# 118 instead of 108 of chunk 0's v rows in its own stage, weight loads ahead of two stores, the last sum in two halves

## What is computed

```python
xn = RMSNorm(h)
experts, gates = top16_of_product_keys(xn @ wq)         # per head: 16 ids, softmax of their scores
act = gelu(einsum('chkd,cd->chk', u_tab[experts], xn))  # 128 dots per token
y   = h + einsum('chk,chkd->cd', gates * act, v_tab[experts])
```

## Time and profile before

| | |
|---|---|
| median of three runs | 2894.3 us |
| the profiled execution | 2897.38 us, of which span 2895.4 us |
| PE busy | 2580.4 us (89%) |
| DVE busy | 2115.7 us (73%) |
| POOL busy | 1982.2 us (68%) |
| ACT busy | 871.6 us (30%) |
| DMA engines, mean | 389 GB/s over the span, 1125.04 MB |
| chain that ended last | PE 36%, DMA 20%, issue 20%, POOL 16%, DVE 5% |

### The profile page before, as it was taken

The page is one execution under the profiler, slowest core; times in us unless marked ns, Lnnn a source line. Parts: engine busy times, 40 slices in busy tenths (PEclk is TensorE's granted clock), DMA queues, the critical chain, the costliest instruction groups (busy, mean ns, idle before and its releaser), DMA issues.

```text
span 2895.4 us, 29720 instructions
## 1 busy us (share of the span) xinstructions
PE 2580.4 (89%) x7557; PEld 1169.3 (40%) x7557; DVE 2115.7 (73%) x5274; ACT 871.6 (30%) x2016; POOL 1982.2 (68%) x2061
## 2 busy tenths in 40 slices
PE   8999978989978898899979998799989999777777
PEld 4544434434523344344523444244523444222222
DVE  5788876967886678777887778777887757744444
ACT  3223331342214421253214521264214631111111
POOL 1026567677777777777777777777777777777775
PEclk9999989999999999999999999999999999999999
DMA  6239999999999999999999999999999999999999
GB/s 241 96 137 383 349 417 378 340 419 419 419 419 412 411 419 419 419 412 414 413 413 406 407 419 419 411 386 417 419 419 403 395 413 419 414 420 419 419 419 370
DMA packets 321344, 1125.04 MB, mean 389 GB/s; under 512 B 35937, under 2 KB 43641, under 8 KB 321176
## 3 DMA queue, kind: packets, MB, share of 16 engines
q0 software_dynamic: 294912, 1073.87, 92.1%
q1 hardware_dynamic: 26248, 49.27, 4.8%
q10 hardware_dynamic: 16, 0.00, 0.0%
HBM read 1114.62 MB, written 8.39 MB: 388 GB/s over the span
## 4 chain that ended last, share of the span: by engine, by line
PE 36%; DMA 20%; issue 20%; POOL 16%; DVE 5%; ACT 2%; POOLq 0%; ACTq 0%; DVEq 0%
PE psum L1720 17%; POOL w_kept L1621 9%; DMA w_kept<-in_peer_u,experts 9%; PE psum L521 9%; DMA ring_v<-in_peer_v,experts 9%; POOL ring_v L1621 7%; PE psum L1129 3%; DMA w_kept<-in_peer_v,experts 2%; PE psum L1103 2%; PE psum L1652 2%; DVE w_kept L2039 2%; PE psum L1680 1%; PE psum L1670 1%; DVE acc L959 0%; PE psum L1147 0%
## 5 line engine op out<-in xcount | busy, mean ns | idle before, releaser
L1720 PE MATMUL psum<-ring_v,diag 128*128 128x512 f32 x3244 | 1562.7, 606 | 248.8 <-DMA ring_v<-in_peer_v,experts 160.9
L2039 DVE CUSTOM_DVE_ANT_0 w_kept<-w_kept,psum 128x1024 f32<-128x1024 f32 x928 | 1125.5, 1218 | 534.9 <-DMA w_kept<-in_peer_u,experts 529.0
L1621 POOL DMA_INDIRECT w_kept<-in_peer_u,experts x928 | 891.7, 961 | 322.1 <-issue 244.2
L1621 POOL DMA_INDIRECT ring_v<-in_peer_v,experts x841 | 809.9, 963 | 276.1 <-issue 222.2
L1720 PEld LDWEIGHTS psum<-ring_v,diag 128*128 128x128 f32 x3244 | 564.8, 190 | 1022.9 <-issue 754.0
L1866 ACT ACTIVATE diag<-ident,weights 128x128 f32<-128x128 f32 x974 | 353.2, 393 | 739.0 <-PE psum L1720 582.3
L1720 PE MATMUL psum<-w_kept,diag 128*128 128x512 f32 x652 | 315.9, 609 | 40.6 <-DMA w_kept<-in_peer_v,experts 24.7
L521 PE MATMUL psum<-w_sb,xnT 128*128 128x512 f32 x640 | 284.6, 600 | 0.8 <-ACT xnT L701 0.8
L470 POOL DMA_INDIRECT w_kept<-in_peer_u,experts x96 | 90.1, 939 | 230.5 <-DVE experts L1389 177.5
L1621 POOL DMA_INDIRECT w_kept<-in_peer_v,experts x183 | 181.6, 992 | 66.0 <-issue 48.3
L1995 DVE SCALAR_TENSOR_TENSOR acc<-conv_in,taps,acc 128x128 f32<-128x128 f32 x720 | 205.0, 347 | 0.0
(11 more groups left out here) (246 smaller groups left out, 1760.7 us busy)
## 6 DMA issues: line engine op xcount, KB each, us to landing
w_kept<-in_peer_u,experts POOLq DMA_INDIRECT x1024, 9.9
ring_v<-in_peer_v,experts POOLq DMA_INDIRECT x841, 10.2
w_sb<-in_w_in SPq DMA_DIRECT2D x4, 2048.0 KB, 17.0
x_in<-in_x SPq DMA_DIRECT2D x8, 512.0 KB, 6.7
w_kept<-in_w_out SPq DMA_DIRECT2D x1, 4096.0 KB, 14.5
h_res<-in_x SPq DMA_DIRECT2D x8, 512.0 KB, 7.2
w_kept<-in_peer_wq SPq DMA_DIRECT2D x2, 2048.0 KB, 10.4
wo_sb<-in_w_out SPq DMA_DIRECT2D x1, 4096.0 KB, 23.6
```

Of the source, the lines that this page charges most:

```text
L1621: nc.gpsimd.indirect_dma_start(slot(kind, n), None, peer_u[0] if kind == "u" else peer_v[0], bass.IndirectOffsetOnAxis(S.experts[c % 2][:, ...
L1720: last = nc.tensor.matmul(y_ps[:, j * BANK:(j + 1) * BANK], diag[:, e % DIAGS, :], slot("v", n)[:, j * BANK:(j + 1) * BANK], start=e == 0, ...
L2039: nc.vector.tensor_tensor_reduce(out=row, in0=row, in1=hn, scale=1.0, scalar=0.0, op0=ALU.mult, op1=ALU.add, accum_out=dots[:, e:e + 1]).t ...
```

## The change

In phase 0, for the last chunk, the two weight loads are issued ahead of `store_h` and `store_q`: `wo_sb` once TensorE has finished group Q (before: G, but behind `store_h`), `wq_sb` once it has finished K. In phase 1, `CAUGHT` becomes 118: ten more v rows of chunk 0 in its own stage, and slots 0 to 9 of stage 1 issue only u rows; v rows 118 to 127 follow in slots 10 to 19. Of chunk 0's v rows 49 instead of 43 go aside, of the last 20 rows of the kernel 10 instead of 7. Chunk 0's head 7 is weighed at slot 47 of its own stage. `end_y` and the last store are made in two halves of 512 columns.

```diff
--- before.py
+++ after.py
@@ -427,6 +427,11 @@
             at = slice(n * BANK, (n + 1) * BANK)
             sp.dma_start(w_kept[:, :, at], peer_wq[0, :, at].rearrange("(k p) n -> p k n", p=P)).then_inc(landed, 16)
         for i in range(2, CHUNKS):
+            if i == LAST:
+                sp.wait_ge(projected[Q], CHUNKS)
+                sp.dma_start(wo_sb[:, :, :], w_out[0].rearrange("(k p) n -> p k n", p=P)).then_inc(S.wo_loaded, 16)
+                sp.wait_ge(projected[K], CHUNKS)
+                sp.dma_start(wq_sb[:, :, :], peer_wq[0].rearrange("(k p) n -> p k n", p=P)).then_inc(S.wq_loaded, 16)
             store_h(i)
             if i == LAST - 2:
                 sp.wait_ge(S.tapped, 2 * TAPS * CB)
@@ -434,12 +439,7 @@
                 sp.dma_start(conv_in[:, :, :], hT_spill[:, :, 2 * P:3 * P + HALO]).then_inc(S.c_in, 16)
             if i < LAST - 1:
                 next_x(i + 1)
-            if i == LAST:
-                sp.wait_ge(projected[G], CHUNKS)
-                sp.dma_start(wo_sb[:, :, :], w_out[0].rearrange("(k p) n -> p k n", p=P)).then_inc(S.wo_loaded, 16)
             store_q(i)
-        sp.wait_ge(projected[K], CHUNKS)
-        sp.dma_start(wq_sb[:, :, :], peer_wq[0].rearrange("(k p) n -> p k n", p=P)).then_inc(S.wq_loaded, 16)
         sp.wait_ge(qT_stored, 16 * CHUNKS)
         sp.wait_ge(hT_stored, 16 * CHUNKS)
 
@@ -1442,15 +1442,15 @@
     side_added = sem("side_added")
     FIRST, TAIL = 0, CHUNKS - 1
     AT_ONCE = 8
-    CAUGHT = ROWS - LAG
+    CAUGHT = 118
     kept = range(EARLY + AT_ONCE, ROWS)
     apart = len(kept) - 0
     u_slot = {e: 2 * n if n < apart else 42 + 4 * (n - apart) for n, e in enumerate(kept)}
     first_u = {at: e for e, at in u_slot.items()}
-    head_ends = {u_slot[(h + 1) * TOPK - 1] + 1: h for h in range(AHEAD, PH - 1)}
+    head_ends = {u_slot[(h + 1) * TOPK - 1] + 1: h for h in range(AHEAD, PH)}
     first_at = {4 + e * (SLOTS - 5) // CAUGHT: e for e in range(CAUGHT)}
-    SIDE = ([row_of(FIRST, e) for e in range(CAUGHT) if (e % 3 != 0 if 30 <= e < 70 else e % 4 == 3)]
-            + [row_of(TAIL, e) for e in range(ROWS - LAG, ROWS) if e % 3 == 0])
+    SIDE = ([row_of(FIRST, e) for e in range(CAUGHT) if (e % 3 != 0 if 30 <= e < 56 else e % 4 != 0 if 56 <= e < 76 else e % 4 == 3)]
+            + [row_of(TAIL, e) for e in range(ROWS - LAG, ROWS) if e % 2 == 0])
     FIRST_SIDES = len([n for n in SIDE if n < ROWS])
     y_side = w_kept[:, KT_D - 2, :]
     in_side = lambda c, e: row_of(c, e) in SIDE
@@ -1494,6 +1494,8 @@
 
         if c == FIRST:
             return (FIRST, first_at[s]) if s in first_at else None
+        if c == FIRST + 1 and s < CAUGHT - (ROWS - LAG):
+            return None
         return (c, s - LAG) if s >= LAG else (c - 1, s - LAG + ROWS)
 
     def rows_in_order():
@@ -1519,7 +1521,10 @@
 
         if c == FIRST and s < SLOTS - LAG + SPREAD:
             return (FIRST, first_at[s + LAG - SPREAD]) if s + LAG - SPREAD in first_at else None
-        return (c, s - SPREAD) if s >= SPREAD else (c - 1, s - SPREAD + ROWS)
+        e = s - SPREAD if s >= SPREAD else s - SPREAD + ROWS
+        if c == FIRST and e < CAUGHT or c == FIRST + 1 and s < SPREAD and e < CAUGHT:
+            return None
+        return (c, e) if s >= SPREAD else (c - 1, e)
 
     def heads_ended(c, s):
 
@@ -1578,8 +1583,11 @@
                 store(c - 1)
 
         over_chunks(step)
-        store(CHUNKS - 1)
-        sp.wait_ge(y_stored, 16 * CHUNKS)
+        for j in range(2):
+            at = slice(j * BANK, (j + 1) * BANK)
+            sp.wait_ge(y_copied, 2 * (CHUNKS - 1) + j + 1)
+            sp.dma_start(out[0, (CHUNKS - 1) * P:, at], y_out[:, at]).then_inc(y_stored, 16)
+        sp.wait_ge(y_stored, 16 * (CHUNKS + 1))
 
     @block.gpsimd
     def _(pool):
@@ -1921,7 +1929,7 @@
         def step(c, f):
             for s in range(SLOTS):
                 if c is not None:
-                    if s == 0 and later(c):
+                    if s == 0 and c > FIRST + 1:
                         gelu(c - 1, PH - 1)
                     for w in heads_ended(c, s):
                         gelu(c, w)
@@ -2077,10 +2085,15 @@
 
         def end_y():
 
-            dve.wait_ge(row_added, pe_rows(CHUNKS * ROWS - 1))
             dve.wait_ge(side_added, len(SIDE))
             dve.wait_ge(y_stored, 16 * (CHUNKS - 1))
-            nc.vector.tensor_tensor(y_out[:, :], y_ps, y_side, ALU.add).then_inc(y_copied, 2)
+            for j in range(2):
+                at = slice(j * BANK, (j + 1) * BANK)
+                if j == 0:
+                    dve.wait_ge(half_added, CHUNKS)
+                else:
+                    dve.wait_ge(row_added, pe_rows(CHUNKS * ROWS - 1))
+                nc.vector.tensor_tensor(y_out[:, at], y_ps[:, at], y_side[:, at], ALU.add).then_inc(y_copied, 1)
 
         def front(f, s):
             a, after = divmod(s - ATT0 - ATT_SUM, ATT_STEP)
@@ -2147,7 +2160,7 @@
                     u, v = u_at(c, s), v_at(c, s)
                     if u is not None:
                         dot_row(c, u)
-                    if s == 1 and later(c):
+                    if s == 1 and c > FIRST + 1:
                         weigh_rows(c - 1, PH - 1)
                     if s:
                         for h in heads_ended(c, s - 1):
```

## The result

The changed kernel takes 2908.7 us (median of five runs, 2905.2 to 2909.6) against 2892.8 for the kernel before (median of five, the three named at the start among them): 1.0045 times its time, 95% interval 1.0034 to 1.0055. By that ratio it is **13 us slower**; the two medians lie 16 us apart, and 27 and 23 further runs of the kernel before, beside the experiments, have medians of 2894.1 and 2894.6 us. The forecast was 2891.4 with a range up to 2898. It was wrong in sign and in range.

What follows compares the result with a forecast made beforehand. It took gathers, paced nearly equally by DMA and POOL, to bound the kernel. On the span, +9.8 - 12.5 + 1.0 - 1.2 = -2.9 us gave a median forecast of 2891.4 us, range 2884 to 2898.

Steps and rivals of the forecast that it cites:

- What bounds the kernel: Whole kernel: DMA and POOL paces nearly equal, 1.25 and 1.24 us a gather; gathers that start earlier shorten it.
- Part 1: Weight loads ahead of the stores, end of phase 0: v row 3 held until 381, v row 12 late by 3.3 us.
- Part 2: Ten more v rows in stage 0: +13.8, -2, +1.8 us; chunk 1 starts 9.8 us later, then -12.5 us for fewer gathers.
- the hole would close: End of stage 0: experts ready at 567.7 just as POOL arrives, first u row of chunk 1 at 569.1.
- Part 3: Slots 0 to 9 of stage 1, u rows alone: waits for dots cost +1 us, between 0 and 5.5.
- Part 4: Head 7 weighed at once: two instructions change place on engines with idle time, worth nothing.
- Part 5: Kernel's end: last add and store in halves, -1.2 us, between 0 and -1.5; the changed rows aside cost nothing.
- The rivals: Four other outcomes: waits vanish 2887.3 (chance 0.29), stores don't wait 2882 (0.05), hole stays 2893.8 (0.09), slower 2904 (0.10).
- the slower one: Rival at v row 3 of chunk 0: `store_h` lands at up to 394, POOL 16 us late, 2904 us; chance 0.10.

Runs made afterwards that it cites:

- e3: The kernel before with only the two weight loads moved ahead of both stores; 2897.4 us, 1.0009 of the kernel before.
- g3: The kernel before with only `wo_sb` ahead of the last `store_h`, `wq_sb` behind both stores, last add and store in halves; 2887.7 us, 0.9975 of the kernel before.
- e1: The changed kernel with all 13 buffers open to v rows from row 44 of chunk 0 instead of 40; 2898.0 us, 1.0011 of the kernel before.
- g4: The kernel before with all 13 buffers open to v rows from row 36 of chunk 0 instead of 40; 2911.8 us, 1.0062 of the kernel before.
- h1: The changed kernel with `wo_sb` ahead of the last `store_h`, `wq_sb` behind both stores, all 13 buffers from row 49; 0.9967 of the kernel before, at some 355 GB/s.
- g2: The changed kernel with all 13 buffers from row 44 and the weight loads behind the stores as before; 2898.3 us, 1.0009 of the kernel before.
- g1: The changed kernel itself, unaltered, run again; 2907.6 us, 1.0042 of the kernel before.

## Why the prediction was wrong, step by step

**What bounds the kernel**: right. Gathers that POOL starts sooner or later are the time: the changed kernel's last v gather starts 8.9 us later than before (2889.88 against 2880.98), its span is 7.7 us longer, and the difference is the 1.2 us of the halves.

**Part 1**: right in size. v row 3 held until 380.61 (forecast 381), v row 12 at 399.70, +4.2 us (forecast +3.3); timed alone it costs 2.6 us (e3). `wq_sb` took 34.5 us from its issue at 343.33 and `store_h` 30.8 from 349.04, so they landed at 377.8 and 379.8. The trace agrees with the rule of the Trainium skill (DMA: Bandwidth & Descriptors, Queues, rings and completion order) that each DMA engine takes the descriptors of one queue in ring order. What I missed is that the order could be halved: with one load ahead of the store (g3) v row 3 is held for 1.57 us and the kernel is faster, with both it is held for 17.39 and the kernel is slower.

**Part 2** is the step that failed. It said that POOL's extra idle in stage 0 "shrinks as POOL comes later than before: -2 us". The two new waits alone are 7.04 + 4.96 - 0.60 = 11.4 us over the usual gaps. From v row 12 to the last v row of the stage, the waits of 0.9 us and more add up to 4.0 us over the gaps before (1.17, 2.53, 1.22) and 12.2 after (with 1.15): **+8.2 us instead of -2**. The other terms were right or better: part 1 +4.2 (forecast +3.3), and what is left for the ten gathers is 12.1, where the sum had 13.8 + 1.8 = 15.6, so that error hid 3.5 us of the other one. Together the last v row starts 24.5 us later (575.48 against 551.00); the forecast had 16.9. I had costed ten gathers, six rows aside and four more on TensorE, and I had asked of the buffers at the start of chunk 1 whose rows they hold. I did not ask it of the other end of the same stretch, although `first_at` and `ALONE` stand in the text: one number, `CAUGHT`, moves row 40 from slot 49 to 45, and the other, 40, stays. So the first gather of chunk 1 started at 577.38 instead of 569.1, 8.3 us off, and e1 gives some 10 us back. g4 puts the same kind of stall into the kernel before, where it costs 18, its third wait included.

The forecast that the hole would close was right: the experts stand at 576.10 and POOL comes just then. It closed because both came late.

**Part 3** was taken too low: +1 us, between 0 and 5.5. The waits at chunk 1's start are 0.96 + 1.68 + 2.66, 4.4 us over the usual gaps, and the stage of chunk 1 became 9.0 us shorter, not 11.5. The last two, 3.7 us over the gaps, are the mechanism I named: u rows 6 and 9 of chunk 1 wait for the dots of rows 0 and 3, whose buffers they take, and h1 has the same two. In e1 and g2 they are absent, and POOL waits for TensorE instead (g2: 7.0 us over the gaps), for the buffers of the last v rows, which I had put "inside the same bound". Without the loads the sum gave the ten rows 9.8 - 3.3 - 12.5 + 1.0 = -5.0 us, and waits of this size are enough to use that up. That the rows would pay without them is not shown.

**Part 4**: nothing, as far as a profile shows. **Part 5**: 1.2 us in the profile, as forecast; not to be timed. **The rivals**: the slower one had its place at v row 3, with a landing at 390. The landing was at 379.8 and the slowness came 80 us later, by another wait.

## What to carry to other kernels

When rows are packed closer in a schedule with a shared ring of buffers, compute for each end of every stretch who held the buffer, and how many gathers lie between; a gather that takes the buffer of the one two before it costs a landing and a use, with the whole in-order queue behind it. A hole at the end of a stage is no stock of time: a stall in the middle delays the engine that ends the hole too. When a load is moved ahead of a store to fill idle DMA time, ask who waits for the store, and count the bytes ahead of it: here 4 MB ahead gained some 7 us (halves of the last sum included), and 8 MB lost 3. Where between them it turns wasn't measured.

## What the runs showed of the hardware that I had not expected

An issue on SP can itself last long. Behind the two weight loads the instruction of `store_h` took 4.19 us and that of `store_q` 11.93, against 0.53 and 0.33 before:

```profile
343.33 0.38 SPq L434 DMA_DIRECT2D wq_sb<-in_peer_wq  x1
349.04 4.19 SPq L398 DMA_DIRECT2D hT_spill<-hT_out  x1
353.27 11.93 SPq L393 DMA_DIRECT2D qT_spill<-qT_out  x1
```

In e1, e3 and g1, with the same order of loads, they took 4.88 to 6.31 and 10.30 to 11.42 us. Why, no run here shows.

And one kernel's time can differ far more than by this change: the kernel before took 2894 us in two sets of runs and 3283 to 3289 in three others, where kernels moved about 355 GB/s instead of 419. One set of each kind has the same chip number on record, so the number of the chip doesn't settle it.
